# One-row zero matmuls on TensorE at two places of every attention unit of a two-block transformer kernel

## The chip, the core and the metric

The kernel runs on one core of a Trainium2 chip. A core has five engines that work side by side and wait for one another through semaphores: TensorE (PE; its weight loads are shown apart as PEld), VectorE (DVE), ScalarE (ACT), GpSimd (POOL) and SyncE (SP). The metric is the device time of one execution, in microseconds (us). TensorE's clock has two levels, 1.2 and 2.4 GHz; the profile gives the granted one as a share of 2.4 GHz, so 0.50 is 1.2 GHz and 1.00 is 2.4 GHz.

## The reference

256 tokens of width 1024 go through a first block with two layers and then through a second block. What matters here is the attention of each:

```python
for l in range(2):                       # first block
    hn = adaln(x, ...); parts = split(hn @ w_in[l])
    o_a = diff_attention(...)            # two softmaxes per head, their difference times v
    o_b = latent_attention(...)
    o_c = indexed_sparse_attention(...)  # an index score picks 64 keys, then softmax
    o_d = chunk_band_attention(...)
    x = x + g_m * (concat(o_a, o_b, o_c, o_d) @ w_out[l])
    x = x + g_f * ffn_or_experts(...)
# second block
x = x + 0.5 * rmsnorm(swiglu(rmsnorm(x)))
q, k, v = rmsnorm(x) @ w_qkv             # 8 heads neighbourhood, 8 heads dilated
x = x + rmsnorm(concat(rmsnorm(o_na), rmsnorm(o_dil)) @ w_out)
x = x + 0.5 * rmsnorm(swiglu(rmsnorm(x)))
```

Every attention is, for four heads and a block of 128 queries: scores q·k, scale and bias, softmax over up to 256 keys, and the probabilities times v.

## The kernel before

One program per engine, written out by hand. Large products (`gemm`, `ffn`, `experts`) take their weights from memory in chunks; ACT and DVE split each chunk into a high and a low half and TensorE does three 512-column matmuls per piece (L528 to L530). Between them stand three stretches of attention: layers 0 and 1 of the first block and one of the second block ("layer 2").

An attention stretch is a list of **units**: one kind of attention, four heads, one block b of 128 queries. Layers 0 and 1 have the kinds A (two units to a block, combined at the second), B, I (index scores, no values), C and D; block 0 sees 128 keys and block 1 sees 256. Layer 2 has N and L, two groups of four heads each, always 256 keys. 24 units in all call `values`: eight a layer.

For unit u and the next one, u+1, the engines do this, each in its own fixed order:

- TensorE: `score(u+1)` (L714, into banks 0 to 3 of the accumulator memory `ps`), at some units `fills` (L637, L673, L679, transposes and products for the next group, each waiting for ACT's copy of the one before), then `values(u)`: wait for the probabilities (`probs`, or `combined` for A), transpose them into banks 4 and 5 (L726, 4 or 8 of them), wait for ACT's copy (`pT_ready`) and for DVE to have taken the result of the unit before out of bank 6 (`mixed`), and multiply by v (L738, 8 or 16 instructions, into columns 0 to 255 of bank 6).
- DVE: bias and row maximum of u+1 (L1452, L1455), `finish(u)`, in layer 0 also a step of the modulation weights (L1278, L1281), then `store(u-1)` (L1512), which raises `mixed`. For I it adds up the scores (L1466) and picks the keys.
- ACT: the exponentials of u+1 (L1089), then the copy of u's transposes (L1096, raises `pT_ready`); for I a relu (L1084).

`clear_y`, at the start of every feed-forward stretch, is older and stays: it multiplies the one-row tile of zeros `zero` (bf16, 1 partition, 128 columns) with 512 columns of one partition, to write zeros into a bank (L556). `finite` is that partition of the constant tile `unit`, read as bf16.

Of the kernel before, what the change touches and what calls it, by code (L numbers as in the profile page):

```python
# [108 lines left out]
def head_slot(h):  # L109

    return (h % 2) * 2 + h // 2
# [114 lines left out]
def program(nc, d):  # L226
    with ExitStack() as ctx:
        def sb(name, shape, dt=F32):
            return ctx.enter_context(nc.sbuf_tensor(name, shape, dt))

        def sem(name):
            return ctx.enter_context(nc.semaphore(name))
# [43 lines left out]
        ps = ctx.enter_context(nc.psum_tensor("ps", [P, 8, 512], F32))  # L276
# [57 lines left out]
        zero = sb("zero", [1, P], BF16)  # L334
        finite = unit[0:1, :].bitcast(BF16)
# [24 lines left out]
        pT_ps, pT_ready, o_ps, mixed = (sem(n) for n in ("pT_ps", "pT_ready", "o_ps", "mixed"))  # L360
# [147 lines left out]
        def _(pe):  # L508
            def mark(s):
# [2 lines left out]
                nc.tensor.matmul(ps[0:1, 7, 0:2], zero[:, 0:1], finite[:, 0:2], start=True, stop=True,  # L512
                                 skip_group_check=True).then_inc(s, 1)

            def transpose_x(t):

                for j in range(4):
                    for kt in (2 * j, 2 * j + 1):
                        for b in range(NB):
                            m = nc.tensor.transpose(ps[:, j, (kt % 2) * T + b * P:(kt % 2) * T + (b + 1) * P],  # L520
                                                    XN[:, b, kt * P:(kt + 1) * P], ident[:, :])
                    m.then_inc(xt_ps, 1)
# [194 lines left out]
            def values(u):  # L717

                src = PR[:, (u.su - 1) % 2 if u.kind == "A" else u.su % 2]
                if u.kind == "A":  # L720
                    pe.wait_ge(combined, u.comb + 1)
                else:
                    pe.wait_ge(probs, u.su + 1)
                for h in range(4):
                    for kb in range(u.nk // P):
                        m = nc.tensor.transpose(ps[:, 4 + h // 2, (h % 2) * T + kb * P:(h % 2) * T + (kb + 1) * P],  # L726
                                                src[:, head_slot(h), kb * P:(kb + 1) * P], ident[:, :])
                m.then_inc(pT_ps, 1)
                pe.wait_ge(pT_ready, u.pu + 1)
                if u.pu >= 1:  # L730
                    pe.wait_ge(mixed, u.pu)
                for h in range(4):
                    for kb in range(u.nk // P):
                        if u.kind == "B":
                            c = B_UKV + h * P + HD
                        else:
                            c = {"A": A_V, "C": C_V, "D": D_V, "N": 2 * D, "L": 2 * D + 512}[u.kind] + (4 * u.g.half + h) * HD
                        m = nc.tensor.matmul(ps[:, 6, h * HD:(h + 1) * HD], PT[:, h, kb, :], PROJ[:, kb, c:c + HD],  # L738
                                             start=kb == 0, stop=kb == u.nk // P - 1)
                m.then_inc(o_ps, 1)  # L740

            def attention(layer):
                us = units_of(layer)
                pe.wait_ge(gemm_out, 2 * sum(GEMM_GROUPS[:2 * layer + 1]))
                fills(us[0].g, 0, us[0].g.n_fills)
                score(us[0])
                for n, u in enumerate(us):
                    part = fill_part(u)
                    if part and last_of_group(u):
                        fills(*part)  # L750
                    if n + 1 < len(us):
                        score(us[n + 1])
                    if part and not last_of_group(u):
                        fills(*part)
                    if u.pu is not None:
                        values(u)
# [108 lines left out]
            for layer in range(LAYERS):  # L865
                chunks = (24, ADA_CHUNKS)[layer]
                mod_columns(0, 2, 6 * layer, (ADA_EARLY, ADA_CHUNKS)[layer])
                pe.wait_ge(xn_ready, 2 * NORM_NO[3 * layer])
                transpose_x(3 * layer)
                pe.wait_ge(xt_ready, 4 * (3 * layer + 1))  # L870
                gemm(2 * layer)
                pe.wait_ge(gemm_out, 2 * sum(GEMM_GROUPS[:2 * layer + 1]))
                attention(layer)
                pe.wait_ge(mixed, pu_end(layer))
                transpose_x(3 * layer + 1)

                pe.wait_ge(ada_used, chunks)
# [5 lines left out]
                gemm(2 * layer + 1)  # L883
                pe.wait_ge(xn_ready, 2 * NORM_NO[3 * layer + 2])
                transpose_x(3 * layer + 2)
                pe.wait_ge(xt_ready, 4 * (3 * layer + 3))
                if layer == 0:
# [1029 lines left out]
```

## Time and profile before

| | |
|---|---|
| median of three runs | 2586.34 us (2583.64 to 2587.12) |
| span of the profiled execution | 2586.1 us |
| TensorE busy | 2179.1 us, 84% |
| mean granted clock | 0.888 |
| attention stretches, us from the span's start | 124 to 278, 626 to 766, 2229 to 2320 |
| TensorE busy in them | 73.49, 76.04, 59.80 us |

The profile is one execution. Its span lies 0.2 us from the median, so what is added to one is added to the other. A row of the timeline merges equal instructions that follow one another; a matmul's end is modelled, with its run through the array in it, so the next may start some 0.1 to 0.2 us before the end that is shown. "Idle before" is counted from that shown end.

### The profile page before, as it was taken

To read this page: it belongs to the slowest core of one execution; us is meant where nothing else is said; L and a number is where in the kernel's file an instruction comes from. 1 tells how busy PE (TensorE), PEld (TensorE's weight loads), DVE (VectorE), ACT (ScalarE), POOL (GpSimd) and SP (SyncE) were. 2 spreads that over 40 slices of the span, in tenths; PEclk is the share of its full clock that TensorE was granted. 3 is DMA by queue.
4 is the path that set the end of the run, shared out by engine and by line. 5 is a ranking of instruction groups with operands and counts; after the bars stand their busy time and mean duration, and the time that the engine had idled before them with its cause. 6 is when DMAs were issued, how large, how long until landed. Compare 5 with 4: busy or idle time off the path is not lost.

```text
span 2586.1 us, 29301 instructions
## 1 busy us (share of the span) xinstructions
PE 2179.1 (84%) x9596; PEld 1761.5 (68%) x9596; DVE 1696.9 (66%) x2035; ACT 1369.9 (53%) x1848; POOL 46.3 (2%) x80
## 2 busy tenths in 40 slices
PE   3854779987647899999999999999978997766997
PEld 3733668866436687878787878787857885655886
DVE  5377377753453797979797979797976554324554
ACT  2422234433321687878787878787863444333443
POOL 1010000000000000000000000000000000000000
PEclk9955689988556899999999999999999998867999
DMA  9433358733003597979797979797964553202451
GB/s 369 163 146 114 107 200 318 306 134 128 1 17 137 229 374 289 372 284 375 286 374 284 375 281 379 278 378 287 372 251 157 184 181 128 81 1 98 179 195 49
DMA packets 80544, 572.69 MB, mean 221 GB/s; under 512 B 9088, under 2 KB 9728, under 8 KB 12272
## 3 DMA queue, kind: packets, MB, share of 16 engines
q1 hardware_dynamic: 70112, 508.59, 51.8%
q0 software_dynamic: 7936, 57.05, 5.9%
q10 hardware_dynamic: 2448, 6.41, 0.7%
q8 instruction: 29, 0.48, 0.1%
q14 instruction: 19, 0.16, 0.0%
HBM read 570.97 MB, written 1.05 MB: 221 GB/s over the span
## 4 chain that ended last, share of the span: by engine, by line
PE 71%; issue 12%; DVE 9%; ACT 6%; DMA 1%; POOL 1%; ACTq 0%; POOLq 0%; DVEq 0%
PE ps L528 20%; PE ps L530 20%; PE ps L529 20%; PE ps L738 2%; PE ps L714 2%; ACT arena L1089 1%; PE ps L807 1%; PE ps L816 1%; PE ps L637 1%; ACT arena L1141 1%; DMA arena<-in_ada 1%; PE ps L791 1%; DVE ps L1452 1%; DVE xt_low L1359 1%; ACT arena L1096 1%
## 5 line engine op out<-in xcount | busy, mean ns | idle before, releaser
L1625 DVE TENSOR_TENSOR weights_low<-ring,weights_high 128x1024 fp32r<-128x1024 f32 x672 | 801.6, 1222 | 68.3 <-ACT weights_high L1125 43.6
L528 PE MATMUL ps<-weights_high,xt_high 128*128 128x512 f32 x1808 | 737.7, 408 | 63.3 <-DVE weights_low L1625 42.3
L1125 ACT ACTIVATE weights_high<-ring 128x1024 fp32r<-128x1024 f32 x672 | 708.2, 1058 | 78.6 <-PE ps L530 70.0
L530 PE MATMUL ps<-weights_high,xt_low 128*128 128x512 f32 x1808 | 719.0, 398 | 0.0
L529 PE MATMUL ps<-weights_low,xt_high 128*128 128x512 f32 x1808 | 718.5, 397 | 0.0
L1366 DVE TENSOR_TENSOR weights_low<-ring,weights_high 128x1024 fp32r<-128x1024 f32 x294 | 357.7, 1224 | 249.0 <-ACT weights_high L960 247.5
L960 ACT ACTIVATE weights_high<-ring 128x1024 fp32r<-128x1024 f32 x294 | 307.2, 1057 | 373.9 <-PE ps L530 359.0
L528 PEld LDWEIGHTS ps<-weights_high,xt_high 128*128 128x128 f32 x1808 | 349.1, 193 | 145.9 <-DVE weights_low L1625 47.3
L530 PEld LDWEIGHTS ps<-weights_high,xt_low 128*128 128x128 f32 x1808 | 347.7, 192 | 75.2
L529 PEld LDWEIGHTS ps<-weights_low,xt_high 128*128 128x128 f32 x1808 | 350.0, 194 | 71.0 <-issue 1.9
L528 PE MATMUL ps<-weights_high,hT_high 128*128 128x512 f32 x712 | 279.2, 392 | 4.2 <-DVE hT_low L1403 4.2
L530 PE MATMUL ps<-weights_high,hT_low 128*128 128x512 f32 x712 | 277.3, 389 | 0.0
L529 PE MATMUL ps<-weights_low,hT_high 128*128 128x512 f32 x712 | 277.0, 389 | 0.0
L528 PEld LDWEIGHTS ps<-weights_high,hT_high 128*128 128x128 f32 x712 | 133.7, 188 | 35.5 <-DVE hT_low L1403 5.0
L530 PEld LDWEIGHTS ps<-weights_high,hT_low 128*128 128x128 f32 x712 | 133.6, 188 | 28.2
L529 PEld LDWEIGHTS ps<-weights_low,hT_high 128*128 128x128 f32 x712 | 133.7, 188 | 27.3
L738 PE MATMUL ps<-arena 128*128 128x64 f32 x320 | 67.8, 396 | 86.4 <-ACT arena L1096 79.5
L738 PEld LDWEIGHTS ps<-arena 128*128 128x128 f32 x320 | 63.6, 302 | 95.4 <-ACT arena L1096 95.4
L1089 ACT ACTIVATE arena<-ps,nmax 128x256 f32<-128x256 f32 (+1 forms) x112 | 47.2, 435 | 138.6 <-DVE nmax L1455 115.9
L520 PE MATMUL ps<-unit,XN 128*128 128x128 f32 x160 | 35.9, 417 | 80.9 <-DVE XN L1333 73.8
L520 PEld LDWEIGHTS ps<-unit,XN 128*128 128x128 f32 x160 | 32.5, 225 | 84.1 <-DVE XN L1333 76.4
L1134 ACT ACTIVATE hT_high<-ps 128x256 fp32r<-128x256 f32 x112 | 43.0, 384 | 77.2 <-PE ps L791 77.2
(194 smaller groups left out, 1536.2 us busy)
## 6 DMA issues: line engine op xcount, KB each, us to landing
ring<-in_stream SPq DMA_DIRECT2D x483, 1024.0 KB, 4.9
Z<-in_ada POOLq DMA_DIRECT2D x42, 1024.0 KB, 5.1
arena<-in_ada POOLq DMA_DIRECT2D x6, 1024.0 KB, 16.2
Z<-in_na POOLq DMA_DIRECT2D x1, 2048.0 KB, 9.7
Z<-in_dil POOLq DMA_DIRECT2D x1, 2048.0 KB, 15.9
band<-in_band ACTq DMA_DIRECT2D x2, 768.0 KB, 18.9
X<-in_x SPq DMA_DIRECT2D x1, 1024.0 KB, 5.1
gate_mix<-in_rows ACTq DMA_DIRECT2D x2, 512.0 KB, 9.6
```

The costliest lines, as they stand in the source:

```text
L520: m = nc.tensor.transpose(ps[:, j, (kt % 2) * T + b * P:(kt % 2) * T + (b + 1) * P], XN[:, b, kt * P:(kt + 1) * P], ident[:, :])
L528: nc.tensor.matmul(out, xh, wh, start=n, stop=False, skip_group_check=True)
L529: nc.tensor.matmul(out, xh, wl, start=False, stop=False, skip_group_check=True)
L530: return nc.tensor.matmul(out, xl, wh, start=False, stop=last, skip_group_check=True)
L714: m = nc.tensor.matmul(out, lhs, rhs, start=True, stop=True)
L738: m = nc.tensor.matmul(ps[:, 6, h * HD:(h + 1) * HD], PT[:, h, kb, :], PROJ[:, kb, c:c + HD], start=kb == 0, stop=kb == u.nk // P - 1)
L960: act.activation(WH[:, p % SPLITS, :], ring[:, chunk % RING, half * PIECE:(half + 1) * PIECE], ACT.Copy).then_inc(hi_ready, 1)
L1089: ins = act.activation(PR[:, par, s, 0:u.nk], src[:, s, 0:u.nk], ACT.Exp, bias=nmax[:, par, s:s + 1], accum_out=den[:, par, h:h + 1])
L1125: act.activation(WH[:, slot, :], raw, ACT.Copy).then_inc(m["hi_ready"], 1)
L1134: act.activation(hTH[:, par].rearrange("p f n -> p (f n)"), ps[:, 6 + par, 0:2 * P], ACT.Copy).then_inc(m["hT_hi"], 1)
L1366: nc.vector.tensor_tensor(WL[:, p % SPLITS, :], ring[:, chunk % RING, half * PIECE:(half + 1) * PIECE], WH[:, p % SPLITS, :].bitcast(F32), ...
L1625: nc.vector.tensor_tensor(WL[:, slot, :], raw, WH[:, slot, :].bitcast(F32), ALU.subtract).then_inc(m["lo_ready"], 1)
```

## The change

At two places of `values`, so 24 times in the program, TensorE does six matmuls of one row of zeros (bf16, 128 columns of weights, 256 columns streamed) into columns 256 to 511 of a bank. The first six go to bank 5 and stand ahead of the wait for the probabilities; the transposes that follow overwrite what is read there. The second six go to bank 6, of which only columns 0 to 255 are ever read. The waits at the second place are split: `mixed` now stands ahead of the six, `pT_ready` behind them. 288 matmuls are added; what is computed stays.

```diff
+            def stay_busy(count, bank):
+                for _ in range(count):
+                    nc.tensor.matmul(ps[:, bank, 256:512], zero[:, :], finite[:, 0:256], start=True, stop=True,
+                                     skip_group_check=True)
...
             def values(u):
                 src = PR[:, (u.su - 1) % 2 if u.kind == "A" else u.su % 2]
+                stay_busy(6, 5)
                 if u.kind == "A":
                     pe.wait_ge(combined, u.comb + 1)
                 else:
...
                 m.then_inc(pT_ps, 1)
-                pe.wait_ge(pT_ready, u.pu + 1)
                 if u.pu >= 1:
                     pe.wait_ge(mixed, u.pu)
+                stay_busy(6, 6)
+                pe.wait_ge(pT_ready, u.pu + 1)
                 for h in range(4):
```

How the instructions stand on TensorE, at two places. First, layer 0, around `values` of B's second block: scores of the first I unit, transposes, values, scores of the next. The changed kernel's lines stand 7 to 9 further down (L721 is L714, L734 is L726, L747 is L738), and L519 is the added matmul. Before:

```order
L714 MATMUL ps<-FS,arena 128x128 [waits probs,filled]
L714 MATMUL ps<-FS,arena 128x128 x3
L726 MATMUL ps<-unit,arena 128x128 [waits probs]
L726 MATMUL ps<-unit,arena 128x128 x7
L738 MATMUL ps<-arena 128x64 [waits mixed,pT_ready]
L738 MATMUL ps<-arena 128x64 x7
```

Now:

```order
L721 MATMUL ps<-FS,arena 128x128 [waits probs,filled]
L721 MATMUL ps<-FS,arena 128x128 x3
L519 MATMUL ps<-unit,zero 128x256 x6
L734 MATMUL ps<-unit,arena 128x128 [waits probs]
L734 MATMUL ps<-unit,arena 128x128 x7
L519 MATMUL ps<-unit,zero 128x256 [waits mixed]
L519 MATMUL ps<-unit,zero 128x256 x5
L747 MATMUL ps<-arena 128x64 [waits pT_ready]
L747 MATMUL ps<-arena 128x64 x7
```

Scores and transposes stood side by side; six added matmuls now stand between them and six more between the transposes and the values, of which the first waits for `mixed`.

Second, the end of layer 2: the values of the last unit but one, and the whole last unit, which has no scores ahead of it. Before:

```order
L738 MATMUL ps<-arena 128x64 [waits mixed,pT_ready]
L738 MATMUL ps<-arena 128x64 x7
L726 MATMUL ps<-unit,arena 128x128 [waits probs]
L726 MATMUL ps<-unit,arena 128x128 x7
L738 MATMUL ps<-arena 128x64 [waits mixed,pT_ready]
L738 MATMUL ps<-arena 128x64 x7
```

Now:

```order
L747 MATMUL ps<-arena 128x64 [waits pT_ready]
L747 MATMUL ps<-arena 128x64 x7
L519 MATMUL ps<-unit,zero 128x256 x6
L734 MATMUL ps<-unit,arena 128x128 [waits probs]
L734 MATMUL ps<-unit,arena 128x128 x7
L519 MATMUL ps<-unit,zero 128x256 [waits mixed]
L519 MATMUL ps<-unit,zero 128x256 x5
L747 MATMUL ps<-arena 128x64 [waits pT_ready]
L747 MATMUL ps<-arena 128x64 x7
```

The transposes of the last unit followed the values before them at once; six added matmuls now come first.

## Rows read from the trace of the kernel before

**Rows 1.** Windows, the three attention stretches: length, busy by engine, then PEclk
```profile
124.00:278.00 154.00, 73.49 (x300) 55.72 (x296) 102.98 (x209) 37.88 (x120) 12.79 (x21) 0.57 0.34 123
626.00:766.00 140.00, 76.04 (x320) 55.97 (x320) 60.46 (x173) 40.36 (x123) 3.02 (x3) 0.56 0.02 5
2229.00:2320.00 91.00, 59.80 (x290) 49.31 (x288) 23.40 (x31) 29.60 (x83) 0.00 (x0) 0.70 0.00 0
```
**Rows 2.** Chain of waits, layer 2, sixth unit to the last: start, us, what
```profile
2302.54 2.03 PE ps L714 x8
...
2304.59 1.25 DVE ps L1452
...
2307.18 1.93 ACT arena L1089 x8
2309.11 0.92 ACT arena L1096
...
2313.76 1.72 PE ps L726 x8
```
**Rows 3.** Timeline, TensorE, layer 2: start, us, what, [idle before <- what ended it]
```profile
2241.70 1.92 PE L726 MATMUL ps<-unit,arena 128*128 128x128 f32 x8
2245.33 2.00 PE L738 MATMUL ps<-arena 128*128 128x64 f32 x16 [1.72 <-ACT arena L1096]
...
2298.86 3.68 PE L738 MATMUL ps<-arena 128*128 128x64 f32 x16 [3.63 <-ACT arena L1096]
...
2316.58 3.67 PE L738 MATMUL ps<-arena 128*128 128x64 f32 x16 [1.11 <-ACT arena L1096]
```
**Rows 4.** Timeline, TensorE, B's second block, layer 0
```profile
203.06 2.02 PE L714 MATMUL ps<-FS,arena 128*128 128x128 f32 x8
204.87 1.80 PE L726 MATMUL ps<-unit,arena 128*128 128x128 f32 x8
207.78 2.00 PE L738 MATMUL ps<-arena 128*128 128x64 f32 x16 [1.11 <-ACT arena L1096]
```
**Rows 5.** Timeline, TensorE, end of layer 0 (values of C's and of D's blocks)
```profile
257.84 3.65 PE L738 MATMUL ps<-arena 128*128 128x64 f32 x16 [2.25 <-DVE XN L1512]
...
269.24 1.94 PE L738 MATMUL ps<-arena 128*128 128x64 f32 x8 [4.70 <-DVE XN L1512]
```
**Rows 6.** Timeline, TensorE, layer 1: first transposes of A; around B's second block
```profile
655.06 1.11 PE L726 MATMUL ps<-unit,arena 128*128 128x128 f32 x4 [0.33 <-DVE arena L1502]
...
705.21 2.00 PE L738 MATMUL ps<-arena 128*128 128x64 f32 x16 [1.11 <-ACT arena L1096]
```
**Rows 7.** Timeline, TensorE, start of a product and of two feed-forward stretches
```profile
50.61 0.80 PE L528 MATMUL ps<-weights_high,xt_high 128*128 128x512 f32 x1 [3.65 <-DVE xt_low L1359]
...
55.89 0.56 PE L528 MATMUL ps<-weights_high,xt_high 128*128 128x512 f32 x1
...
345.80 1.88 PE L556 MATMUL ps<-unit,zero 1*128 1x512 bf16 x4 [3.65 <-DVE xt_low L1359]
347.61 0.79 PE L528 MATMUL ps<-weights_high,xt_high 128*128 128x512 f32 x1
...
2379.77 1.88 PE L556 MATMUL ps<-unit,zero 1*128 1x512 bf16 x4 [3.37 <-DVE xt_low L1359]
```
**Rows 8.** Windows: the two feed-forward starts, one-column matmuls, two stretches in attention
```profile
346.00:353.00 7.00, 7.00 (x17) 4.51 (x16) 6.82 (x6) 0.00 (x0) 0.57 (x1) 0.50 0.49 167
...
353.30:360.00 6.70, 6.70 (x31) 5.55 (x30) 1.23 (x1) 2.24 (x2) 0.53 (x1) 1.00 0.70 289
...
2380.00:2387.00 7.00, 7.00 (x17) 4.55 (x16) 1.99 (x2) 0.00 (x0) 0.00 (x0) 0.50 0.38 150
...
290.40:297.40 7.00, 6.94 (x32) 6.90 (x32) 0.00 (x0) 0.00 (x0) 0.00 (x0) 0.50 0.00 0
...
704.90:714.90 10.00, 8.38 (x58) 7.29 (x60) 3.89 (x15) 3.99 (x6) 0.00 (x0) 1.00 0.00 1
...
2244.20:2247.40 3.20, 2.07 (x18) 2.00 (x20) 0.00 (x0) 1.08 (x3) 0.00 (x0) 1.00 0.00 0
```

## The prediction

> **What bounds the kernel now.** I read the windows of the three attention stretches first, since the change touches nothing else. They last 154, 140 and 91 us, 385 of 2586.1, and the granted clock in them is 0.57, 0.56 and 0.70 [rows 1]: of its two levels, 1.2 GHz most of the time. TensorE is busy for about half to two thirds of them. Then the chain of waits [rows 2]: in layer 2 each link hands over without slack, scores (2.03 us), DVE's bias (1.25) and its maximum, ACT's exponentials (1.93) and copy (0.92), then the values (3.68 in [rows 3]). TensorE is on the chain with scores and values, and off it with the transposes, except in the last unit, where these (1.72) follow the values and the copy waits for them. DVE and ACT do not depend on TensorE's clock. So a faster clock would pay on scores and values only, and anything put in TensorE's queue costs nothing only while DVE and ACT have the turn.
>
> **What six added matmuls take.** The nearest row is the older product of one row of zeros: four of 512 columns from 345.80, with the next matmul at 347.61 [rows 7], so 0.45 us each at 1.2 GHz. Half the columns at the same pace is 0.23 us, six of them 1.35 us; if the time did not fall with the columns it would be 2.7, if the weight loads overlapped better 1.2. [...] At 2.4 GHz it would be some 0.7.
>
> **The first six, ahead of the wait for the probabilities.** They cost nothing where TensorE then waits longer than 1.35 us, or where the transposes they delay have slack before ACT's copy. In layer 2 the four units without fills have that slack: the values of such a unit start after an idle time of 3.63 us [rows 3], which 1.35 of the first and 1.35 of the second six do not fill. So do A's other three units and C's first block, where TensorE waits for DVE for several us. It is not free in these:
> - Where transposes follow TensorE's own work and ACT's copy waits for them: B's second block in layers 0 and 1 and the last unit of all three layers. There the idle time before the values is 1.11 us, which is the copy alone (three of the five stand in [rows 3, 4, 6]). Five times 1.35, and 0.1 each since the second six outlast the 1.11 slightly: 7.2 us.
> - Where the slack is short. A's first transposes in layer 1 wait 0.33 us [rows 6]; counted from the true end of the work before, the dummies cost 0.8. In layer 2 the units with fills have 1.7 us before the values [rows 3], against 2.7 of added work with part of the transposes already ahead of ACT: about 0.9 each for three. C's second block in layer 1: 0.2. Together 3.7 us.
>
> **The second six, ahead of the copy's wait.** The copy with its exponentials hides them in most units. But `mixed` now stands ahead of them, and whatever waits for it is pushed by 1.35 us. In layer 0, where DVE also works on the modulation weights between bias and store, `mixed` is what the values wait for twice, after 2.25 and 4.70 us idle [rows 5]: 2 x 1.35 = 2.7 us. Behind TensorE there stand the next scores and then DVE's bias, so it passes on. For B's first block `mixed` comes about 1 us before the copy: 0.2 in each of two layers. Together 3.1 us. Bounds of these direct terms, 14.0 us in all: 10 if the small ones are absorbed by ACT, 20 if a dummy takes a third more.
>
> **What the clock does.** Is a one-row product work to the clock? In a product stretch that begins with 128-row matmuls at 50.61 the pace changes within the matmul at 55.89, 5.3 us later. Two feed-forward stretches begin with four one-row matmuls, at 345.80 and 2379.77, with no gap behind them [rows 7]; the clock is 0.50 in all of 346 to 353 and of 2380 to 2387 although TensorE is busy in every microsecond [rows 8]. In the first it is 1.00 from 353.3 on [rows 8]: 7.2 to 7.5 us after the first one-row matmul, but 5.4 to 5.7 after the first 128-row one at 347.61, close to the 5.3 of the product stretch: as though the one-row ones had not been there. The same is seen where TensorE is busy for 6.94 of 7.00 us with one-column products and stays at 0.50 [rows 8]. So I expect the dummies not to raise the clock.
>
> They may even lower it. It is at 1.00 in stretches that follow an unbroken run of 128-row work: after the scores and transposes at 203.06 to 206.7 in layer 0, whose values then take 2.00 us instead of 3.68 [rows 3, 4]; likewise in layer 1, from 704.9 to 714.9; and at 2244.2 to 2247.4 in layer 2 [rows 3, 6, 8]. The change puts 1.35 us of one-row products into the middle of each of these runs. Each loss is 3.68 − 2.00 = 1.7 us for the values; in layer 1 the scores and fills up to 714.9 lose too, and the nearest measure is layer 0, which has them at 1.2 GHz: another 1.6; in layer 2 the scores behind add 0.3. 1.7 + 3.3 + 2.0 = 7.0 us. Bounds: 0 (the runs are still dense enough) and 10 (one more such run, at the third unit of layer 2, goes too).
>
> **Sum:** 14.0 + 7.0 = 21.0 us on 2586.1, on the median 2586.34 as well: 2607.3 us. What follows an attention stretch begins with products that wait for it, so I let nothing be given back.
>
> **Two rules of the skill.** The Trainium skill (TensorE: Matmul & The Clock Gate, "Why this matters for your kernels") advises to keep TensorE continuously busy and free of idle gaps so that the full clock holds; taken literally it favours the change, and would give the first rival below. The rows of one-row and one-column work above speak against the literal reading. The same page (Part 4) says that transposes do not count as busy; by that the runs I fear to break would not have raised the clock, and the sum would be 2600.3. The trace differs: the full clock at 2244.2 comes right behind twelve transposes and nothing else [rows 3, 8].
>
> **Rivals.** (1) *The zeros do count*, and the clock stays at 2.4 GHz through the attention. For it: TensorE is counted busy during them, and two starts are thin evidence. Then some 14 of the 24 sets of values, those on the chain at 1.2 GHz, save 1.7 us each, and as many scores 0.9 (a bit less than half of 2.03), 36 us, and the dummies cost half of 14: 2586 − 36 + 7 = 2557 us. It decides as soon as the clock in 2229 to 2320 goes from 0.70 to near 1. This is the faster side. (2) *Only the direct costs*, the clock as before: 2600.3 us. It holds if a run may have a hole in it. (3) *Everything is hidden*: the direct terms are small because the added matmuls run into each other and end before the 1.11 us copy, and the first six overlap the work before them; at most 5 us: 2590 us. Against it stands that the transposes at 204.87 follow the scores without any gap.
>
> **How the numbers follow.** Forecast 0.52; (2) 0.26; a larger clock loss than mine, up to 2618, 0.06; (3) 0.07; (1) 0.09. The range leaves out (1) and part of (3) and of the top: 2592 to 2616. A measurement of this kernel can tell some 0.2% (5 us) from no change. Faster by more than that: 0.09, within it 0.06, slower 0.85.
>
> **What would show it.** In the changed profile: 24 pairs of six one-row matmuls, each six about 1.3 us long; the clock in the three stretches at 0.57, 0.56, 0.70 or lower; the values behind B's second block at 3.7 us and not 2.0 in layers 0 and 1; the wait for `mixed` now on the added matmuls in C's and D's blocks of layer 0; the three stretches longer by about 7, 7 and 6 us, and the rest unchanged but for a us or two. I am wrong if the clock in these stretches rises, or if the last unit of each layer is not longer by 1.4 us.

## The result, and the profile after

The changed kernel takes 2606.36 us (median of four runs, 2605.25 to 2606.9) against 2584.99 us before (four runs, 2583.53 to 2587.12). The ratio is 1.0081, with a 95% interval of 1.0069 to 1.0094: 21 us slower, where 21 were forecast. The profiled execution has a span of 2604.2 us, 18.1 more than that of before, so its own readings have to add up to 18 and not to 21; the two spans lie 2.2 us under the median (the changed kernel) and 1.1 us over it (the kernel before).

The page of the changed kernel, part 1:

```profile
PE 2248.5 (86%) x9884; PEld 1796.4 (69%) x9884; DVE 1696.9 (65%) x2035; ACT 1370.3 (53%) x1848; POOL 46.3 (2%) x80
```

TensorE has 288 matmuls more and is 69 us longer "busy" (2179.1 before), and DVE and ACT have the instructions they had. The windows of the three attention stretches (length, busy time by engine, then granted clock), which answer to [rows 1]:

```profile
125.00:287.00 162.00, 98.11 (x396) 67.78 (x392) 103.14 (x209) 37.98 (x120) 12.77 (x21) 0.54 0.32 117
634.00:782.00 148.00, 100.53 (x414) 69.60 (x414) 60.80 (x173) 40.65 (x124) 3.02 (x3) 0.54 0.02 5
2247.00:2341.00 94.00, 79.17 (x384) 58.74 (x384) 23.82 (x32) 29.88 (x84) 0.00 (x0) 0.63 0.00 1
```

TensorE is busy for 98 of 162 us where it was for 73 of 154, and the clock did not rise: 0.54, 0.54, 0.63 against 0.57, 0.56, 0.70. The stretches are 8, 8 and 3 us longer.

The timeline of TensorE around B's second block in layer 0, which answers to [rows 4]. In the attention the profile has two records for each score and each product of the values, so four scores stand as x8 and eight products as x16, and one for each transpose or added matmul. L721, L734 and L747 are L714, L726 and L738 of before, L519 is the added matmul:

```profile
204.48 2.02 PE L721 MATMUL ps<-FS,arena 128*128 128x128 f32 x8
206.43 1.46 PE L519 MATMUL ps<-unit,zero 1*128 1x256 bf16 x6
207.82 1.97 PE L734 MATMUL ps<-unit,arena 128*128 128x128 f32 x8
209.72 1.46 PE L519 MATMUL ps<-unit,zero 1*128 1x256 bf16 x6
211.10 3.67 PE L747 MATMUL ps<-arena 128*128 128x64 f32 x16
```

Six added matmuls take 1.38 to 1.39 us from the first's start to the next instruction's (206.43 to 207.82), 0.23 each. There is no idle time left before the values, and these take 3.67 us instead of 2.00. The granted clock under the values of B's second block in both layers:

```profile
211.10:214.70 3.60, 3.60 (x18) 3.60 (x18) 0.28 (x1) 0.00 (x0) 0.53 (x1) 0.50 0.35 127
715.40:719.00 3.60, 3.60 (x18) 3.60 (x18) 0.00 (x0) 0.00 (x0) 0.00 (x0) 0.50 0.02 5
```

The end of layer 0, which answers to [rows 5]:

```profile
262.34 1.46 PE L519 MATMUL ps<-unit,zero 1*128 1x256 bf16 x6 [0.76 <-DVE XN L1521]
263.73 3.67 PE L747 MATMUL ps<-arena 128*128 128x64 f32 x16
...
275.07 1.46 PE L519 MATMUL ps<-unit,zero 1*128 1x256 bf16 x6 [3.22 <-DVE XN L1521]
276.46 1.97 PE L747 MATMUL ps<-arena 128*128 128x64 f32 x8
```

The wait for `mixed` (DVE's L1521, L1512 before) stands on the added matmuls now, and the values come 1.39 us behind its end, where they came at once.

Where the 18 us are, read from the starts of the values (L738, L747) and of the products (L528, L535) in both traces; a row that goes "to the last values" goes to their end:

| stretch | before | after | more |
|---|---|---|---|
| start of the span to the first product | 50.6 | 50.5 | −0.1 |
| first product to values of B's first block, layer 0 | 150.7 | 152.2 | 1.5 |
| from there to C's first block (holds B's second) | 49.3 | 52.4 | 3.2 |
| from there to the last values, layer 0 | 27.1 | 31.5 | 4.4 |
| on to the product before layer 1 | 279.6 | 278.3 | −1.3 |
| on to the first values, layer 1 | 101.5 | 102.1 | 0.6 |
| from there to the values of B's first block, layer 1 | 39.9 | 39.9 | 0.0 |
| values of B's first block to C's first, layer 1 | 40.8 | 45.5 | 4.7 |
| from there to the last values, layer 1 | 26.5 | 28.8 | 2.3 |
| on to the product before layer 2 | 1396.3 | 1398.3 | 2.0 |
| on to the first values of layer 2 | 83.2 | 84.4 | 1.2 |
| first to last values of layer 2 | 74.9 | 76.2 | 1.3 |
| rest | 265.8 | 264.0 | −1.8 |

### The profile page after: what moved, and what is told of

Read it like the earlier page. It is cut to its first block, busy times and chain, and to the rows that moved or that the text cites. A ratio compares the mean times of both kernels' runs of the same rounds, so it can differ in the third digit from the quotient of the medians.

```text
span 2604.2 us, 29854 instructions
## 1 busy us (share of the span) xinstructions
PE 2248.5 (86%) x9884; PEld 1796.4 (69%) x9884; DVE 1696.9 (65%) x2035; ACT 1370.3 (53%) x1848; POOL 46.3 (2%) x80
## 4 chain that ended last, share of the span: by engine, by line
PE 72%; issue 12%; DVE 9%; ACT 5%; DMA 1%; POOL 1%; ACTq 0%; POOLq 0%; DVEq 0%
PE ps L535 20%; PE ps L537 20%; PE ps L536 20%; PE ps L747 2%; PE ps L721 2%; PE ps L816 1%; ACT arena L1098 1%; PE ps L825 1%; ACT arena L1150 1%; DMA arena<-in_ada 1%; PE ps L800 1%; PE ps L644 1%; PE ps L519 1%; DVE ps L1461 1%; PE ps L734 1%
## 5 line engine op out<-in xcount | busy, mean ns | idle before, releaser
L535 PE MATMUL ps<-weights_high,xt_high 128*128 128x512 f32 x1808 | 736.9, 408 | 63.3 <-DVE weights_low L1634 42.3
L535 PEld LDWEIGHTS ps<-weights_high,xt_high 128*128 128x128 f32 x1808 | 348.3, 193 | 145.7 <-DVE weights_low L1634 47.3
L535 PE MATMUL ps<-weights_high,hT_high 128*128 128x512 f32 x712 | 279.2, 392 | 4.2 <-DVE hT_low L1412 4.2
L535 PEld LDWEIGHTS ps<-weights_high,hT_high 128*128 128x128 f32 x712 | 133.7, 188 | 35.4 <-DVE hT_low L1412 5.0
L527 PE MATMUL ps<-unit,XN 128*128 128x128 f32 x160 | 36.1, 419 | 82.0 <-DVE XN L1342 74.9
L747 PE MATMUL ps<-arena 128*128 128x64 f32 x320 | 71.2, 410 | 37.7 <-ACT arena L1105 37.7
L747 PEld LDWEIGHTS ps<-arena 128*128 128x128 f32 x320 | 66.8, 316 | 48.2 <-ACT arena L1105 46.9
```

What stands on the lines that cost most here:

```text
L535: nc.tensor.matmul(out, xh, wh, start=n, stop=False, skip_group_check=True)
```

## The experiments

**Does the clock see work of more rows?** The same 288 matmuls, type, columns and places, with 128 rows of zeros against 128 rows of the constant tile (the older uses keep their one row).

```diff
-        zero = sb("zero", [1, P], BF16)
+        zero = sb("zero", [P, P], BF16)
...
-                    nc.tensor.matmul(ps[:, bank, 256:512], zero[:, :], finite[:, 0:256], ...)
+                    nc.tensor.matmul(ps[:, bank, 256:512], zero[:, :], unit[:, 0:P].bitcast(BF16), ...)
```

> Both sets of six, but of 128 rows of zeros with 256 columns of the constant tile, where the change has one row: the same number of matmuls, columns, type and place. My theory (the clock does not see one-row work, but would see 128-row work): the granted clock in the three attention stretches rises from about 0.56, 0.56, 0.70 to above 0.85, values take 2.00 us in most units, and the time falls below the kernel before, 2550 to 2575 us. Rival A (zeros, or bf16, or matmuls that nobody reads do not count, whatever their rows): the time and the clock stay as with one row, 2606 us. Rival B (the hole in a run did not matter, the change costs its own time alone): as A or as mine, it does not say.

Measured: 2571.85 us, ratio to before 0.9942 (0.9923 to 0.9960): 15 us *faster* than before by the ratio (13 by the medians), and some 34 faster than with one row. Windows of the three stretches, as above:

```profile
124.00:276.00 152.00, 85.82 (x392) 62.78 (x392) 103.08 (x209) 37.88 (x120) 12.76 (x21) 0.60 0.36 125
623.00:759.00 136.00, 83.76 (x416) 60.95 (x416) 60.69 (x173) 40.82 (x124) 3.02 (x3) 0.65 0.02 5
2223.00:2309.00 86.00, 62.78 (x387) 50.30 (x385) 23.83 (x32) 29.82 (x84) 0.00 (x0) 0.82 0.00 1
```

Around B's second block in layer 0, with six of 128 rows at both places, the values take 2.00 us:

```profile
204.42 1.49 PE L519 MATMUL ps<-unit,zero 128*128 128x256 bf16 x6
205.70 1.91 PE L734 MATMUL ps<-unit,arena 128*128 128x128 f32 x8
...
208.73 2.00 PE L747 MATMUL ps<-arena 128*128 128x64 f32 x16 [0.43 <-ACT arena L1105]
```

Shown: the number of matmuls, the type and the zeros are not what keeps the clock down; the rows are. Rival A is out. The time came out as expected, the clock did not: 0.60, 0.65 and 0.82, not above 0.85. In layers 0 and 1 six matmuls do not fill waits of up to 15 us; in layer 2 the values of the first five units take 2.00, 3.65, 2.00, 3.68 and 2.00 us. The second and third unit of its timeline:

```profile
2246.28 0.83 PE L519 MATMUL ps<-unit,zero 128*128 128x256 bf16 x6 [1.58 <-DVE XN L1521]
2248.68 3.65 PE L747 MATMUL ps<-arena 128*128 128x64 f32 x16 [1.57 <-ACT arena L1105]
...
2260.16 2.00 PE L747 MATMUL ps<-arena 128*128 128x64 f32 x16 [1.24 <-ACT arena L1105]
```

**Which of the two places costs?** First the first six alone, with the waits of the second place as before:

```diff
-                if u.pu >= 1:
-                    pe.wait_ge(mixed, u.pu)
-                stay_busy(6, 6)
                 pe.wait_ge(pT_ready, u.pu + 1)
+                if u.pu >= 1:
+                    pe.wait_ge(mixed, u.pu)
```

> Only the first six, ahead of the wait for the probabilities; the waits of the second place as before the change. My sum: direct terms of the first place about 8.5 us (five times 1.35 on the chain, 1.8 for short slack) and the whole clock term of about 7 us, since it is the first six that stand between scores and transposes: +15 us on the kernel before, 2600 us. Rival (direct costs only, no clock term): +8.5, 2593.5 us.

Measured: 2602.0 us, ratio 1.0063 (1.0048 to 1.0077), that is 12 to 20 us more; 15 were expected, and the rival's 8.5 lies outside. In its timeline the values of B's second block in layer 0 wait for the copy as before, and take 3.67 us:

```profile
205.28 1.46 PE L519 MATMUL ps<-unit,zero 1*128 1x256 bf16 x6
206.66 1.97 PE L734 MATMUL ps<-unit,arena 128*128 128x128 f32 x8
209.74 3.67 PE L746 MATMUL ps<-arena 128*128 128x64 f32 x16 [1.11 <-ACT arena L1104]
```

Then the second six alone, with the wait for `mixed` ahead of them:

```diff
                 src = PR[:, ...]
-                stay_busy(6, 5)
                 if u.kind == "A":
```

> Only the second six, with the wait for mixed ahead of them. My sum: 3.1 us for the waits for mixed (2 x 1.35 in layer 0, 0.2 twice) and five times 0.1: +3.6 us on the kernel before, 2588.5 us, and no clock term, since scores and transposes stand side by side. If the costs were simply shared by the number of matmuls, half of 21: 2595.5 us.

Measured: 2587.95 us against 2584.4, ratio 1.0006 (0.9995 to 1.0017): 1.3 less to 4.4 us more. The expected 3.6 lies within, a half share of the change's 21 does not. So the first place carries most of the cost (12 to 20 us). One thing went another way than expected: scores and transposes of B's second block stand side by side here, yet in layer 0 the values behind took 3.68 us, while in layer 1 they took 2.00:

```profile
203.12 2.02 PE L721 MATMUL ps<-FS,arena 128*128 128x128 f32 x8
204.93 1.91 PE L733 MATMUL ps<-unit,arena 128*128 128x128 f32 x8
...
208.16 3.68 PE L746 MATMUL ps<-arena 128*128 128x64 f32 x16
...
710.33 2.00 PE L746 MATMUL ps<-arena 128*128 128x64 f32 x16
```

**Is there a clock term at all?** The change, without the first six in the five units where I put them on the chain.

```diff
-                stay_busy(6, 5)
+                if not ((u.kind == "B" and u.b == 1) or u is units_of(u.layer)[-1]):
+                    stay_busy(6, 5)
```

> The change, but without the first six in five of the 24 units: B's second block in layers 0 and 1 and the last unit of each layer, where the transposes are on the chain. My theory: it gives back 5 x 1.35 = 6.8 us of direct cost and the clock's 1.7 in layer 0 and 3.3 in layer 1, since the run of scores and transposes at B's second block is whole again: 2606.4 - 11.8 = 2594.6 us, with the values of those two units at 2.00 us. Rival (direct costs only): 2599.6 us, and those values stay at 3.67.

Measured: 2592.87 us, ratio 1.0026 (1.0015 to 1.0036), that is 4 to 9 us above before: 30 of 288 matmuls left out give back 13.5 of 21.4 us by the medians. Own time alone (6.8) would leave 2599.6, a ratio of about 1.006; that is out. It stays out when the price of a set is taken from the run with the first six alone, where the last unit of layer 2 grew by 1.57 us (8.07 between its values and those before, against 6.50): five times that is 7.9, a ratio of 1.0055. My 2594.6 is a ratio of 1.0039 and lies just above the interval: a little more came back than I had summed. The timelines of the two units, layer 0 and layer 1, show the other part:

```profile
205.66 1.67 PE L735 MATMUL ps<-unit,arena 128*128 128x128 f32 x8
207.26 0.82 PE L519 MATMUL ps<-unit,zero 1*128 1x256 bf16 x6
208.44 2.00 PE L748 MATMUL ps<-arena 128*128 128x64 f32 x16 [0.36 <-ACT arena L1106]
...
709.98 2.00 PE L748 MATMUL ps<-arena 128*128 128x64 f32 x16 [0.36 <-ACT arena L1106]
```

**Is the price set by number or by place?** The change in six of the 24 units only, where TensorE waits for DVE anyway.

```diff
+                hidden = u.kind == "A" or (u.kind == "C" and u.b == 0)
+                if hidden:
                     stay_busy(6, 5)
...
+                if hidden:
                     stay_busy(6, 6)
```

> One-row matmuls as in the change, both sets, but only in six of the 24 units: A's (four) and C's first block (two), where TensorE waits for DVE anyway. My theory (the price is set by place, not by number): +0.8 us for A's first transposes in layer 1, 2585 us, no difference that can be measured. Rival (each added matmul costs its share of 21.4 us): 72 of 288, +5.4 us, 2590 us.

Measured: 2586.95 us against 2585.61, ratio 1.0004 (0.9995 to 1.0013), at most 3.4 us: place, not number. A quarter of the matmuls, and no difference that can be measured.

**How many rows?** Both sets of 64 rows. The edit is against the 128-row kernel:

```diff
-  zero[:, :], unit[:, 0:P].bitcast(BF16)
+  zero[0:64, :], unit[0:64, 0:P].bitcast(BF16)
```

> Both sets of six everywhere, with 64 rows instead of 1 or 128. My theory (the clock sees rows, not the fact of a matmul): between the two, 2580 to 2600 us, the clock in the three stretches between that of 1 and of 128 rows. Rival (any matmul with more than a few rows counts in full): 2572 us, as with 128. Rival (only full rows count): 2606 us.

Measured: 2604.96 us, ratio 1.0069 (1.0053 to 1.0084), the same as with one row within the intervals. The stretches have a clock of 0.54, 0.55 and 0.69:

```profile
124.50:285.50 161.00, 97.48 (x392) 68.19 (x392) 102.56 (x209) 37.99 (x120) 12.75 (x21) 0.54 0.32 118
632.00:780.00 148.00, 100.62 (x416) 70.28 (x416) 60.38 (x173) 40.52 (x124) 3.02 (x3) 0.55 0.02 5
2246.00:2338.00 92.00, 75.09 (x384) 57.52 (x384) 23.40 (x31) 29.20 (x83) 0.00 (x0) 0.69 0.00 1
```

My "between the two" was wrong: half the rows brought at most 0.06 of clock in layer 2 and nothing that can be measured in time. The rival that only full rows count gives the time; whether 64 rows count for half and that was too little here, or not at all, stays open.

**A version that beats both.** 128 rows, with the five first sets left out (the 128-row kernel with this edit):

```diff
-                stay_busy(6, 5)
+                if not ((u.kind == "B" and u.b == 1) or u is units_of(u.layer)[-1]):
+                    stay_busy(6, 5)
```

> 128-row matmuls at both places, as in the run with both sets of 128 rows (2571.9 us), but without the first six in B's second block of layers 0 and 1 and in the last unit of each layer. My theory: scores and transposes stand side by side there again, 128-row work both, so the clock loses nothing, and 5 times 0.8 to 1.5 us come off the chain: 2565 to 2569 us. Rival (the first six at these units are what keeps the clock up for the values behind): 2572 to 2577 us.

Measured: 2566.76 us, ratio 0.9915 (0.9900 to 0.9929). As expected, and the rival (2572 to 2577) is out: 128-row work of the kernel itself does there what the dummies would do. Then, on top of it, twelve in place of six at the second place of layer 2's units without fills:

```diff
-                stay_busy(6, 6)
+                stay_busy(12 if u.layer == 2 and not fill_part(u) and u is not units_of(2)[-1] else 6, 6)
```

> As the 128-row run with five first sets left out, but 12 instead of 6 matmuls at the second place of layer 2's units without fills (four of them), where the 128-row run still waits 1.57 us for the copy. My theory: the clock is at its upper level for the values of the second and fourth unit too, which took 3.65 and 3.68 us there: 1.7 us for each and 0.9 for the scores behind: 3 to 5 us below the run with six. Rival (the clock there is set by the stretch before): no gain, or 0.2 us per unit lost where the twelve outlast the copy.

Measured: 2561.79 us, ratio 0.9894 (0.9878 to 0.9910), 5 us below the run before by the medians, though the two intervals overlap a little. In the profiles the stretch from the first values to the end of the last in layer 2, the only one with an edit, went from 68.4 to 60.6 us. A window of 66 us in layer 2 and the second and fourth unit, first with six, then with twelve:

```profile
2227.00:2293.00 66.00, 51.74 (x304) 41.26 (x303) 17.97 (x25) 22.62 (x68) 0.00 (x0) 0.77 0.00 1
...
2240.43 3.60 PE L748 MATMUL ps<-arena 128*128 128x64 f32 x16 [1.56 <-ACT arena L1106]
...
2261.02 3.67 PE L748 MATMUL ps<-arena 128*128 128x64 f32 x16 [1.56 <-ACT arena L1106]
```

```profile
2229.00:2295.00 66.00, 52.18 (x374) 42.71 (x374) 18.76 (x27) 23.91 (x69) 0.00 (x0) 0.90 0.00 1
...
2242.65 2.00 PE L748 MATMUL ps<-arena 128*128 128x64 f32 x16 [0.91 <-ACT arena L1106]
...
2260.93 2.00 PE L748 MATMUL ps<-arena 128*128 128x64 f32 x16 [0.91 <-ACT arena L1106]
```

The clock is 0.90 where it was 0.77, and the time is 23.8 us below the 2585.61 of the kernel before (27 by the ratio).

## Why the prediction was right, point by point

**Price of six: right.** 1.38 us at 1.2 GHz against 1.35.

**Where the first six are not hidden: right in place, a little small.** The last unit of each layer grew by 1.8 us between its values and those before (4.8 to 6.6 in layers 0 and 1, 6.5 to 8.3 in layer 2), where 1.45 were summed. The mis-sized term is what comes on top of the first six: I counted 0.1 us, and it is 0.4. Of that 0.25 is the second six outlasting the copy (from the transposes to the values 3.03 us before, 3.28 now); the rest stands between the values before and the transposes, whose starts were 1.73 us apart in layer 0 and are 3.29 apart now, 0.17 more than the six themselves. A's first transposes in layer 1 come 1.0 us later behind the products ahead of them (starts 2.41 us apart before, 3.39 now), forecast 0.8; the 0.6 in the table has 0.3 us in it that the stretch before them was shorter.

**The wait for `mixed`: right.** The six take 1.39 us there, and the distance to the values before grew by 1.3 us each at C's second and D's first block in layer 0 (7.3 to 8.6, 11.4 to 12.7); with the last unit that stretch grew by 4.4, where 2.7 and 1.45 and small parts gave 4.2.

**Is one-row work seen by the clock: right, it is not**, and shown by the exchange of rows alone. The argument rested on two starts of feed-forward stretches; it held.

**The clock as a loss: right in layers 0 and 1, half right in layer 2.** The stretches that hold B's second block grew by 3.2 and 4.7 us; 1.45 + 1.7 and 1.45 + 3.3 were summed, 3.15 and 4.75. That closeness is partly luck. The distance from the values of B's first block to those of its second, the direct part, grew by 1.9 and 1.8 us; what is left for the clock is 1.3 in layer 0 and 3.0 in layer 1. In both the values lose 1.67. Behind them the chain goes through the next scores and the fills to DVE. In layer 0 the second set of these fills took 0.66 us where it had taken 1.12, which gave 0.4 back; in layer 1 scores and fills lost 1.3 of the 1.6 that I had summed, because the second set was at the upper level again (0.66). Whether such a run brings the clock up depends on when it comes and not on its order alone: with six one-row or 64-row matmuls in the middle of it (the change, the first six alone, 64 rows) the values behind took 3.7 us in 6 of 6 cases, and with the run whole (before, second six alone, five left out, hidden places only) they took 2.0 us in 6 of 8. The two exceptions are both in layer 0. One is the second six alone, where six one-row matmuls stand ahead of the values of B's first block too. The other is the run with the hidden places only: from A's last values on it has the instructions and nearly the gaps of the kernel before, 0.6 us earlier, and its values take 3.65 us where [rows 4] has 2.00:

```profile
202.47 2.02 PE L721 MATMUL ps<-FS,arena 128*128 128x128 f32 x8
204.29 1.91 PE L736 MATMUL ps<-unit,arena 128*128 128x128 f32 x8
207.41 3.65 PE L750 MATMUL ps<-arena 128*128 128x64 f32 x16 [1.20 <-ACT arena L1108]
```

The profiled executions of these two runs are also the slowest of theirs (2592.98 and 2590.15 us against medians of 2587.95 and 2586.95). So the hole is shown to cost in layer 1; in layer 0 the kernel before was at its upper level by a chance of timing that small shifts also take away.

In layer 2 the loss at the first unit came: 3.67 us instead of 2.00 and 0.3 for the scores behind, the 2.0 that were forecast. But the fifth unit gained nearly as much, 2.00 us where before it had 3.67. That is no chance of one profile: in all four runs with six one-row or 64-row matmuls at the first place of layer 2's units (the change, the first six alone, five left out, 64 rows) the first unit is at 3.7 us and the fifth at 2.0, and in the three without them (before, the second six alone, hidden places only) it is the other way round. The forecast had no term for a gain. Why the fifth gains stays open. The units with fills cost less too: 0.9 us each was summed for three, and the third and fifth cost nothing that can be read. The third had 2.55 us idle ahead of its values before, not 1.7. So the stretch from first to last values grew by 1.3 us only, and layer 2 by 2.5 in all, where some 6 were forecast. The first unit, the fifth and the last in the changed kernel, and then the fifth before:

```profile
2263.95 3.67 PE L747 MATMUL ps<-arena 128*128 128x64 f32 x16
...
2307.47 2.00 PE L747 MATMUL ps<-arena 128*128 128x64 f32 x16 [0.89 <-ACT arena L1105]
...
2336.47 3.67 PE L747 MATMUL ps<-arena 128*128 128x64 f32 x16
```

```profile
2287.64 3.67 PE L738 MATMUL ps<-arena 128*128 128x64 f32 x16 [1.72 <-ACT arena L1096]
```

The row at 2336.47 is the last unit, with its 1.11 us of idle time gone.

**The total: right, and closer than the parts.** By these readings the clock cost 1.3 + 3.0 + 2.0 − 1.7 = 4.6 us, where 7.0 were summed. The stretches between the attentions moved by −1.3, +2.0 and −1.8 us without any edit in them, and 1.2 us of the 1.5 from the first product to B's first block stand ahead of the first added matmul; these cancel nearly. So the profiles show 18.1 us where 21.0 were forecast, and the difference is layer 2's. The medians show 21.4. The profiled pair does not explain the 3 us between; executions of one kernel differ by more (the 38 of the kernel before that were timed beside the experiments took 2580.4 to 2592.6 us, the fastest with a mean clock of 0.892 and the slowest with 0.885). That the forecast met the medians to 0.4 us is luck; that it lies within a few us is not.

**The rivals.** That the zeros count (1) is refuted for one row; its mechanism was sound, though, and with 128 rows, 30 of them left out at the five places and 24 put on top in layer 2, it gave 24 of the 29 us that I had put on it. Direct costs only (2) is refuted by the first six alone and by the five left out. All hidden (3) is out by the result.

**The two rules cited.** The advice of the Trainium skill to keep TensorE busy (TensorE: Matmul & The Clock Gate, "Why this matters for your kernels") holds for 128-row work and not for one-row or 64-row work in these runs. What the Trainium skill says of transposes, that they do not count as busy as other matmuls do (the same page, Part 4), is not what this kernel shows: the full clock at 2244.2 stands right behind transposes [rows 3, 8]. The fills ahead of those in [rows 3], transposes as well, took 1.11 us behind an idle time of 5.01, the pace of 1.2 GHz:

```profile
2240.79 1.11 PE L637 MATMUL ps<-unit,arena 128*128 128x128 f32 x4 [5.01 <-ACT arena L1043]
```

In all three runs without added matmuls at this place the values behind took 2.0 us, and with six of one or 64 rows between fills and transposes 3.7 in all four.

## What to carry to other kernels

A matmul that is put in to keep the clock up has to look like the work it stands in for: of 1, 64 and 128 rows only 128 helped here, and numbers between 64 and 128 were not tried. The busy share of TensorE in a profile does not tell; read the granted clock of the stretch. Put it only where the engine waits longer than it takes, never between two pieces of real work that stand side by side, and look at which semaphore wait it now stands behind.

## What the runs showed of the hardware that I had not expected

- Six matmuls of one row take longer than six of 128 rows of the same columns and type at 1.2 GHz: 1.38 us (209.72 to 211.10 in the changed kernel) against 1.28 (204.42 to 205.70 in the 128-row run). Here the cost was not lower for less work.
- 64 rows of 128 gave 2604.96 us and 128 rows 2571.85: the step is not proportional.
- Whether a stretch gets the upper level can turn on a shift of 0.6 us in when it comes, with the same instructions ahead of it (scores at 203.06 and values of 2.00 us in the kernel before, 202.47 and 3.65 in the run with the hidden places only), so a single stretch of one profile is not a sure reading of it.
- The added matmuls took the upper level from layer 2's first unit and gave it to the fifth, in four of four runs. The effect of a hole on the clock is not only a loss at the hole.
